# Choosing the next expert arm in a block of its own, ahead of the return through the experts' outputs, with a marked branch for each pair of widths

## The reference, cut to what matters

```python
def swiglu(h, w_gate, w_up, w_down):
    return (jax.nn.silu(h @ w_gate) * (h @ w_up)) @ w_down

def moe_swiglu(h, router, w_gate, w_up, w_down):
    logits = (h @ router).astype(jnp.float32)
    probs = jax.nn.softmax(logits, axis=-1)
    vals, idx = lax.top_k(probs, TOP_K)
    wts = vals / jnp.sum(vals, axis=-1, keepdims=True)
    combine = jnp.sum(jax.nn.one_hot(idx, N_EXPERTS, dtype=jnp.float32) * wts[..., None], axis=-2)
    out = jnp.zeros_like(h)
    for e in range(N_EXPERTS):
        out = out + combine[..., e:e + 1] * swiglu(h, w_gate[e], w_up[e], w_down[e])
    return out
```

## Time and profile before

| | us |
|---|---|
| median of 3 executions | 1502.63 (1499.26 to 1503.55) |
| the profiled execution | 1501.99 |
| its span, first to last instruction | 1500.1 |
| PE busy | 1439.2 (96%) |
| granted TensorE clock, mean | 0.984 of full speed |
| ring loads moved | 467.92 MB, mean of all DMA 318 GB/s |

### The profile page before, as it was taken

One profiled execution on the slowest core, in us unless ns is written; L12 is line 12 of the kernel. 1 busy time (PEld: TensorE's weight loads), 2 busy tenths in 40 slices (PEclk: granted clock), 3 DMA queues, 4 the chain that ended last, 5 costly groups with the idle time before them and its releaser, 6 DMA issues.

```text
span 1500.1 us, 22480 instructions
## 1 busy us (share of the span) xinstructions
PE 1439.2 (96%) x9384; PEld 926.3 (62%) x9384; DVE 374.8 (25%) x644; ACT 249.3 (17%) x487; POOL 42.1 (3%) x54
## 2 busy tenths in 40 slices
PE   5989999999999979999999999998999999999996
PEld 3446598884498556455369963555996464553462
DVE  3567543420156432121010100211010111210212
ACT  3136210000110022121010000221000121210221
POOL 1000000000000012000000000000000000000000
PEclk9999999999999979999999999999999999999999
DMA  9862577760759539999997766899988899999996
GB/s 376 363 241 93 224 291 270 294 238 29 272 210 354 212 136 387 420 419 421 421 371 280 263 243 234 326 422 418 420 325 290 290 413 421 419 420 421 398 422 254
DMA packets 69071, 476.98 MB, mean 318 GB/s; under 512 B 9475, under 2 KB 9811, under 8 KB 12144
## 3 DMA queue, kind: packets, MB, share of 16 engines
q1 hardware_dynamic: 64768, 467.92, 78.2%
q0 software_dynamic: 3920, 6.53, 1.3%
q10 hardware_dynamic: 288, 1.05, 0.2%
HBM read 478.66 MB, written 2.12 MB: 320 GB/s over the span
## 4 chain that ended last, share of the span: by engine, by line
PE 87%; DMA 5%; DVE 4%; SPq 2%; issue 1%; ACT 1%; DVEq 0%
PE ps L1399 24%; PE ps L1441 16%; PE ps L1376 14%; PE ps L1172 10%; PE ps L1145 8%; PE ps L1223 5%; DMA ring<-stream 5%; DVE acc L625 2%; PE ps L1471 2%; PE ps L1362 2%; SPq L262 1%; PE ps L969 1%; PE ps L1067 1%; PE ps L1306 1%; PE ps L1029 1%
## 5 line engine op out<-in xcount | busy, mean ns | idle before, releaser
L1399 PE MATMUL ps<-ring,hTe 128*64 128x256 f32 (+1 forms) x3584 | 360.5, 384 | 6.7 <-issue 5.2
L1399 PEld LDWEIGHTS ps<-ring,hTe 128*64 128x64 f32 (+1 forms) x3584 | 215.7, 131 | 129.3 <-issue 21.0
L1441 PE MATMUL ps<-ring,aT 128*64 128x512 f32 (+2 forms) x1232 | 285.6, 596 | 3.0 <-DMA ring<-stream 1.7
L1376 PE MATMUL ps<-hTe,ring 128*128 128x144 f32 (+1 forms) x1792 | 212.7, 282 | 7.2 <-issue 7.2
L1376 PEld LDWEIGHTS ps<-hTe,ring 128*128 128x128 f32 x1792 | 212.3, 193 | 8.9 <-issue 8.9
L1441 PEld LDWEIGHTS ps<-ring,aT 128*64 128x64 f32 (+2 forms) x1232 | 97.0, 139 | 181.3 <-issue 173.3
L899 DVE TENSOR_TENSOR aT<-hT,ps 128x512 f32<-128x512 f32 x112 | 77.0, 688 | 515.4 <-ACT hT L531 515.4
L1172 PE MATMUL ps<-hT,ring 128*128 128x256 f32 (+1 forms) x832 | 153.4, 347 | 0.0
L531 ACT ACTIVATE hT<-ps 128x512 f32<-128x512 f32 x112 | 66.9, 597 | 514.0 <-PE ps L1399 307.9
L1172 PEld LDWEIGHTS ps<-hT,ring 128*128 128x128 f32 x832 | 138.1, 191 | 15.7 <-issue 1.0
L1145 PE MATMUL ps<-ring,aT 128*128 128x512 f32 x240 | 104.5, 594 | 0.0
(11 more groups left out here) (186 smaller groups left out, 687.6 us busy)
## 6 DMA issues: line engine op xcount, KB each, us to landing
ring<-stream SPq DMA_DIRECT2D x444, 1024.0 KB, 13.0
gg<-norm_w POOLq DMA_DIRECT2D x4, 512.0 KB, 8.9
x<-x_in SPq DMA_DIRECT2D x1, 1024.0 KB, 5.0
hTe<-ctx_in SPq DMA_DIRECT2D x1, 1024.0 KB, 21.1
rows_store<-xn POOLq DMA_DIRECT2D x1, 1024.0 KB, 4.4
out<-x ACTq DMA_DIRECT2D x2, 512.0 KB, 2.6
aT<-dft POOLq DMA_DIRECT2D x1, 512.0 KB, 8.1
aT<-rope POOLq DMA_DIRECT2D x1, 256.0 KB, 6.0
```

The lines of the kernel that those rows point to most:

```text
L1376: last = pe.matmul(ps[:, 2 * (u % 2) + b, g * SEQ:g * SEQ + width], w, hTe[:, k, 0:width], start=(k == 0), stop=(k == KD - 1))
L1399: last = pe.matmul(to, hTe[:, k, s0:s0 + n], w, start=(k == 0), stop=(k == KD - 1))
L1441: last = pe.matmul(ps[n * r:n * (r + 1), 4 + bank, :], a_T, w[:, f, half * BANK:(half + 1) * BANK], start=(j < max(1, tiles // 2)), stop=( ...
```

## The change

`turn_expert`, `combine` and the choice stand in a new function `leave(width, e)` that is called behind `down`.

- One branch (L1339) separates the last expert from the others, in place of the `If` and of the branch at the loop's end.
- The 16 transposes come first. Behind them the code is filled up to the start of a block of 256 (`addr_align(FETCH, offset=0, max_nops=0)`): the filling is skipped by one branch.
- The six compares follow at the start of that block, ahead of `combine`. They go to one of seven pieces `from{width}to{following}`, one for each successor, which stand right behind in the program.
- A piece begins with a hint instruction that names the branch at the piece's end, then does `combine`, adds one to `at`, and branches to the arm. The last expert has a piece of its own without a hint.
- The alignment that lets each arm start a block is kept, now behind the last expert's piece.

`TURN_AFTER` was 6, the last unit of `down`, so the transposes keep their place behind the last product of `down`. The matmuls and their number are the same.

```diff
-            def enter_arm(name):
+            def choose(name, arm):
                 for i, width in enumerate(WIDTHS[:-1]):
-                    pe.br_eq(which, i, on_true=f"arm{width}", on_false=f"{name}_not{width}")
+                    pe.br_eq(which, i, on_true=f"{arm}{width}", on_false=f"{name}_not{width}")
                     nc.switch_bb(f"{name}_not{width}")
-                pe.addr_align(256, offset=255, max_nops=0)
-                pe.br(f"arm{WIDTHS[-1]}")
+
+            def leave(width, e):
+                pe.br_lt(at, E - 1, on_true=f"leave{width}", on_false=f"last{width}")
+                with nc.body(f"leave{width}", parent=program, valid_engines=on_pe):
+                    turn_expert(e)
+                    pe.addr_align(FETCH, offset=0, max_nops=0)
+                    choose(f"leave{width}", f"from{width}to")
+                    pe.br(f"from{width}to{WIDTHS[-1]}")
+                for following in WIDTHS:
+                    with nc.body(f"from{width}to{following}", parent=program, valid_engines=on_pe):
+                        ahead = pe.mark_branch_hint_location()
+                        combine(e, width)
+                        pe.reg_alu(at, at, 1, ALU.add)
+                        pe.br(f"arm{following}").branch_hint(ahead)
+                with nc.body(f"last{width}", parent=program, valid_engines=on_pe):
+                    combine(e, width)
+                    pe.addr_align(FETCH, offset=FETCH - 1, max_nops=0)
+                    pe.br("experts_done")
...
-                    if d == TURN_AFTER:
-                        with pe.If(e < E - 1):
-                            turn_expert(e)
...
                     next_width()
                     down(e, width)
-                    combine(e, width)
-                    pe.reg_alu(at, at, 1, ALU.add)
-                    pe.br_lt(at, E, on_true=f"after{width}", on_false="experts_done")
-                    nc.switch_bb(f"after{width}")
-                    enter_arm(f"after{width}")
+                    leave(width, e)
```

More of the change, by code:

```diff
@@ L47 @@
 WIDE = 2
-TURN_AFTER = NFE // 4 - 1
+FETCH = 256
 BLOCKS = {64: [(0, 64)], 96: [(0, 64), (64, 32)], 128: [(0, 128)], 144: [(0, 128), (128, 32)],
@@ L1481, in _ @@
             next_width()
-            enter_arm("first")
+            choose("first", "arm")
+            pe.addr_align(FETCH, offset=FETCH - 1, max_nops=0)
+            pe.br(f"arm{WIDTHS[-1]}")
             for width in WIDTHS:
```

## The result

| | before | changed |
|---|---|---|
| median, 14 runs each | 1501.53 us (1498.37 to 1505.31) | 1506.24 us (1502.75 to 1510.61) |
| profiled execution | 1501.99 | 1508.64 |
| its span | 1500.1 | 1506.8 |

The ratio is 1.0031 with a 95% interval of 1.002 to 1.0042. The change makes the kernel slightly slower. The loss is as large as the 0.3% that the prediction names as the bound of what can be told.

The account below looks back on a forecast made before the run. PE is 96% busy, so time comes from its gaps (12.4 us at five seams, waiting for code), its clock or the weight stream; 1501.99 us with -5.7 + 1.6 + 5.6 - 2.4 + 3.9 = +3.0 gives 1505 us, range 1498 to 1512.

Parts of the forecast that it names:

- the central term: Passage from one expert's arm to the next, seams 2, 3, 4, 5, 7: hints start code fetches earlier, -5.7 us.
- What bounds the kernel: PE 96% busy; 12.4 us of gaps at five seams between experts' arms, lower clock behind two, weight stream nearly full.
- What the hint gives, -5.7: Seams 2, 3, 4, 5, 7: the target's fetch starts at the hint, so arms start earlier, together -5.7 us.
- the second fetch, +1.6: Seams 2, 4, 5, 7: the fetch on entering the choice's block runs beside the hint's; half of 0.8 us each, +1.6.
- the first rival: The hint does nothing: only compares saved, -1.2 us, seams 1 and 6 still lose 5.6; 1510 us, chance 0.25.
- The prediction's own test: Branches at the pieces' ends: under 5 us if right; still 5 to 6 us if the hint does nothing.
- The rule of the Trainium skill: Taken branches: prefetch is purely sequential, a target not next costs about 6 us; by it the hint would do nothing.
- Seams 1 and 6, +5.6: From 64 to 96 columns: the choice's block comes between, so the next arm is fetched later; 2.8 us gaps, +5.6 us.
- The clock, -2.4 + 3.9: Granted PE clock: seam 7 regains 2.9 us less a stream wait, -2.4; new gaps at seams 1 and 6 cost +3.9.
- The sum: Whole kernel: -5.7 + 1.6 + 5.6 - 2.4 + 3.9 = +3.0 us on 1501.99, giving 1505 us.
- Where the filling ends: Seam 3, 144 columns: transposes end at 2304, no spare; rival, one instruction later: 4.7 us above forecast, 1510 us, chance 0.14.
- The remark at the end: All seams: if all are closed, the order of fetches was wrong altogether and the time is near 1487 us.

## Why the prediction came out as it did

The time was inside the range and the central term was wrong.

**What bounds the kernel: right.** The gaps are waits for code at branches to blocks that aren't there. With hints that work all are gone, and so is the low clock behind them.

**What the hint gives, -5.7, and the second fetch, +1.6: wrong.** "I take the first, because the instruction has no other use" is the step that failed. Its use depends on where it stands, and behind the compare that chose the piece it had none; why, is open. In place of -4.1 us the five seams gave -1.05 us. The sum is near the -1.2 of the first rival, but not seam by seam: -0.37, -0.85, +0.38, -0.24 and +0.03 us for its -0.5, -0.1, -0.4, -0.1 and -0.1. Most of it is the gap of seam 3, whose branch took 4.94 us instead of 5.97. The second fetch showed a price only at seam 4, where the branch took 6.39 us (6.46 without hints) instead of 6.03. The prediction's own test said so, branches that take 5 to 6 us still. The rule of the Trainium skill that was weighed there (Runtime: NRT & Kernel Launch, section Instruction fetch mechanics: prefetch is sequential) gave the right result for this kernel. As a rule it does not hold in these runs: with the hint 7.7 us ahead the branch to a far block took 0.44 us.

**Seams 1 and 6, +5.6: right**, measured 2.47 + 2.70 = 5.2 us, and 5.0 to 5.4 us in each of the five other profiled executions that have the choice's block in that place (2.65 and 2.63 us in the version without hints).

**The clock, -2.4 + 3.9: wrong in size and place.** It gave +2.7 for a forecast +1.5. Seam 7 kept its gap and won 1.3 us, since its low stretch was milder; seams 1 and 6 lost 3.4, seam 2 another 1.7, and seam 4 won 1.0. I took 2.9 us for a low stretch from one row; here it is 1.5 to 1.7, and other executions show up to 3.0 (0.57 of full clock over 7 us).

**The sum.** In the profiled execution 5.2 - 1.05 + 2.7 gives +6.8 instead of +3.0, which would be 1509. The median of 14 runs is 2.4 us below the profiled one. So the 1505 is near 1506.24 in part by luck. The first rival, 1510 us, had the mechanism at the branches right, and is nearer to the profiled 1508.64.

**Where the filling ends: right** in the count of 2304 (one instruction more opened a gap), wrong in its price, 1.4 us for 4.7.

**The remark at the end**, that closing all seams would give about 1487 us, was near the 1488.84 measured, though not by the change at hand.

## What to carry to other kernels

A branch to code that isn't there costs 5 to 6 us of the sequencer, and a hint removed it when it was given 7.7 us or more ahead. Given 1.4 to 2.5 us ahead it shortened it in part, and behind the compare that chose the piece, 0.5 to 2.1 us ahead, it did nothing. Before work is moved to make room for an earlier decision, look whether the decision is known anyway: here the next width was in a register before `down`, and a chain of six hints there, with no block moved, brought 12 us. And a block put between two neighbours in the code takes from them a fetch that had come free.

## What the runs showed of the hardware

- A hint instruction takes 0.03 to 0.05 us. With enough lead it cut a taken branch to a far block from 5.2 to 6.1 us to 0.30 to 0.45.
- One fetch can take the place of another: with the hints ahead of `down` the queue moved one packet between 1000 and 1014 us, with the hint and its branch in one block two, and both kernels had all seams closed.
- Two fetches can lie side by side. In the full stream a lone packet took 1.1 us, rarely up to 1.6; the later of two that overlapped took 1.8 to 2.3.
- At seams 2, 4 and 7 a long branch ended 1.3 to 1.6 us behind the end of its target's packet, with hints and without.
- Granted clock: the eight executions that have gaps at the seams have 35 of 2.5 to 4.5 us. Behind 26 the mean over the next 7 us was 0.57 to 0.79 of full clock; behind the nine others, of 2.5 to 3.3 us, it was full, and so it was behind every gap of 1.8 us and less.
